# Turned cache pages for the compression stage of a decoder-layer kernel

## The reference, cut to what matters

```
sub = kv[:, :n_sub * 16].reshape(b, n_sub, 16, 2, 2, 64)            # 16 tokens j of each sub-block n
for r in range(2):
    part_r = einsum("bnjcgd,cjde->bncge", sub + pe_r, cmp_w[:, 16 r : 16 r + 16])[:, r:r + n_cmp]
blk = part_0 + part_1                                                # 127 blocks of a sequence, 31 of the prompt
kc, vc = rmsnorm(blk[:, :, 0], gain), blk[:, :, 1]
```

## Time and profile before

| what | us |
|---|---|
| median of three runs | 1944.69 |
| time of the profiled execution | 1945.8 |
| its span | 1943.9 |
| end of stage 1 (last ACT work) | 183.3 |
| stage 2, first SP issue to last PE work | 184.5 to 300.2 |
| PE busy, 185 to 300.4 | 111.1 |
| POOL busy, 185 to 300.4 | 7.5 |

### The profile page before, as it was taken

The page is one execution under the profiler, slowest core; times in us unless marked ns, Lnnn a source line. Parts: engine busy times, 40 slices in busy tenths (PEclk is TensorE's granted clock), DMA queues, the critical chain, the costliest instruction groups (busy, mean ns, idle before and its releaser), DMA issues.

```text
span 1943.9 us, 40081 instructions
## 1 busy us (share of the span) xinstructions
PE 1807.3 (93%) x16517; PEld 970.7 (50%) x16517; DVE 577.7 (30%) x1401; ACT 366.2 (19%) x791; POOL 376.9 (19%) x434
## 2 busy tenths in 40 slices
PE   7998996778899999988999999999999999999992
PEld 4546984554478887443434444443444444343431
DVE  2223324356401111253222313232222313232324
ACT  3232442355400000110111111111111111111110
POOL 0010101137500000601121222222121212222222
PEclk9997997889799999987999999999999999999996
DMA  8205933550051110223999999999999999999986
GB/s 298 102 11 208 404 106 135 213 201 1 26 202 55 55 43 23 113 111 154 404 428 420 418 423 414 424 426 422 419 419 419 413 427 415 423 418 415 423 351 237
DMA packets 59185, 535.47 MB, mean 275 GB/s; under 512 B 15825, under 2 KB 20785, under 8 KB 44114
## 3 DMA queue, kind: packets, MB, share of 16 engines
q1 hardware_dynamic: 47465, 483.30, 60.9%
q0 software_dynamic: 11664, 51.42, 6.7%
HBM read 518.26 MB, written 28.39 MB: 281 GB/s over the span
## 4 chain that ended last, share of the span: by engine, by line
PE 52%; DMA 1%; DVE 1%; issue 0%; POOL 0%; SPq 0%; POOLq 0%; ACT 0%; DVEq 0%
PE psum L2727 34%; PE psum L2753 17%; DMA arena<-y_of 1%; DMA arena<-scr_h,arena 1%; PE psum L2737 0%; DVE arena L2714 0%; DVE arena L2720 0%; POOL arena L2626 0%; DMA y_of<-arena 0%; DVE arena L2719 0%; SPq L2574 0%; DVE arena L2663 0%; SPq L2576 0%; POOL arena L2596 0%; POOLq L2535 0%
## 5 line engine op out<-in xcount | busy, mean ns | idle before, releaser
L2727 PE MATMUL psum<-arena 128*32 128x512 f32 x6144 | 668.3, 592 | 3.6 <-DVE arena L2663 2.4
L2727 PEld LDWEIGHTS psum<-arena 128*32 128x32 f32 x6144 | 210.0, 108 | 442.9 <-issue 438.5
L2753 PE MATMUL psum<-arena 128*32 128x256 f32 x6144 | 343.8, 378 | 0.0
L2753 PEld LDWEIGHTS psum<-arena 128*32 128x32 f32 x6144 | 211.8, 109 | 134.0 <-issue 12.6
L2688 DVE TENSOR_TENSOR arena<-psum,arena 128x512 f32<-128x512 f32 x96 | 66.4, 692 | 576.5 <-PE psum L2727 543.9
L2613 POOL DMA_INDIRECT y_of<-arena x96 | 96.9, 1009 | 475.3 <-ACT arena L2649 475.3
L2376 PE MATMUL psum<-arena 128*128 128x272 f32 x768 | 183.0, 396 | 1.6 <-PEq L224 1.6
L2376 PEld LDWEIGHTS psum<-arena 128*128 128x128 f32 x768 | 146.9, 191 | 35.3 <-issue 3.2
L2645 ACT ACTIVATE arena<-arena 128x256 f32<-128x256 f32 x96 | 40.1, 418 | 611.2 <-DVE arena L2690 598.3
L745 PE MATMUL psum<-arena 128*128 128x512 f32 (+3 forms) x320 | 112.2, 509 | 0.2 <-DVE arena L617 0.2
L2592 POOL DMA_INDIRECT arena<-scr_h,arena x96 | 98.9, 1030 | 48.9 <-POOL arena L2588 28.1
(11 more groups left out here) (360 smaller groups left out, 1544.9 us busy)
## 6 DMA issues: line engine op xcount, KB each, us to landing
arena<-in_w_gu SPq DMA_DIRECT2D x64, 4096.0 KB
arena<-in_w_down SPq DMA_DIRECT2D x32, 4096.0 KB
arena<-in_w_gb SPq DMA_DIRECT2D x24, 512.0 KB, 3.5
arena<-y_of SPq DMA_DIRECT2D x8, 1024.0 KB, 14.2
arena<-in_w_tok SPq DMA_DIRECT2D x3, 2048.0 KB, 17.6
arena<-in_x_all SPq DMA_DIRECT2D x8, 512.0 KB, 11.1
arena<-in_cache_mem SPq DMA_DIRECT2D x8, 512.0 KB, 11.7
arena<-in_cache_win SPq DMA_DIRECT2D x8, 512.0 KB, 11.8
```

The lines of the kernel that those rows point to most:

```text
L2727: mm = pe.matmul(gu_bank(g)[32 * j:32 * j + 32].rearrange("p (h n) -> p h n", h=2), xgT[:, g, 32 * k:32 * k + 32], gu_w(slot)[:, part, :, ...
L2753: mm = pe.matmul(dn_half(g)[32 * j:32 * j + 32], actT[:, g, 32 * k:32 * k + 32], dn_w(slot)[:, part, 256 * j:256 * j + 256], start=(k == 0 ...
```

## The change

The cache in HBM is laid out by page, turned: row (page, a, d) of 1 KB holds (c j g m), with m the eight sub-blocks of the page. The 128 rows of a page are then 128 partitions, and a sequence is 16 pages of 128 rows of 1 KB. The columns that a product reads are 32 runs of 8 words, 256 words apart between pages. No turn on PE and no copy to `kvT` is left for the sequences; the prompt's rows still go that way.

SP issues 9 of the 16 pages of each sequence, each with a row number read into a register from SBUF; POOL issues the other 7 as indirect transfers. There are three buffers (the third lies behind the page numbers, where stage 1's pooling data and `kvT` were), and for each buffer two semaphores. Sequences 0 and 1 are issued in stage 1: by SP between L482 and the writes of the tables, by POOL at the old place.

```diff
+PAGES = PAST // PAGE
+PAGE_W = 2 * PAGE
+BY_SP = 9
-    cc = a["cache_cmp_kv"][0].reshape(-1, SUB // 2, 2, 2, 2, HD)
-    f["cache_cmp"] = cc.transpose(0, 3, 1, 4, 2, 5).reshape(-1, ROWF)
+    cc = a["cache_cmp_kv"][0].reshape(-1, PAGE // SUB, SUB // 2, 2, 2, 2, HD)
+    f["cache_cmp"] = cc.transpose(0, 3, 6, 4, 2, 5, 1).reshape(-1, PAGE_W)
+    f["page_list"] = np.asarray(a["page_table"]).reshape(1, -1)
...
+        sub_buf = lambda s: sub_rows[:, s % 3] if s % 3 < 2 else arena[:, third_at:third_at + ROWF]
+        page_of = lambda buf, pg: buf[:, PAGE_W * pg:PAGE_W * pg + PAGE_W]
+        def load_pages(sp, s):
+            for pg in range(BY_SP):
+                at = PAGES * s + pg
+                first = sp.value_load(page_row[0:1, at:at + 1], min_val=0, max_val=n_rows - 128)
+                sp.dma_start(page_of(sub_buf(s), pg), i["cache_cmp"][bass.ds(first, 128)]).then_inc(s_sub[s % 3], 16)
+        def gather_pages(pool, s):
+            for pg in range(BY_SP, PAGES):
+                at = PAGES * s + pg
+                pool.indirect_dma_start(page_of(sub_buf(s), pg), None, i["cache_cmp"],
+                                        bass.IndirectOffsetOnAxis(page_row[:, at:at + 1], 0)).then_inc(s_subw[s % 3], 16)
...
                 sp.dma_start(pages, i["pages"]).then_inc(s_pg, 16)
+                sp.dma_start(page_list, i["page_list"].partition_broadcast(128)...).then_inc(s_pg, 16)
...
+                sp.wait_ge(s_ix, 2)
+                for s in range(2):
+                    load_pages(sp, s)
                 for h in range(NH):            # the writes of the tables
...
+                dve.tensor_scalar(page_row, page_list, float(PAGE), cols[:, 0:1], ALU.mult, ALU.add).then_inc(s_ix, 1)
```

```diff
+                tokens(0)          # waits for all parts of sequence 7 and the prompt's rows
+                blocks(NS - 1)
+                tokens(1)
+                keys(NS - 1)
+                for c in range(2):
+                    products(NS, c)
                 blocks(NS)
                 keys(NS)
```

More of the change, by code:

```diff
@@ L312, in build_program @@
         row_index = take(NS, dt=U32)
+        page_row = take(NS * PAGES, dt=U32)
+        after_pages = cursor[0]
         u_prompt = take(2, 16 + NP_TOK)
@@ L336, in build_program @@
         s_ix = sem("s_ix")
-        s_sub = [lasting(f"s_sub{n}") for n in range(2)]
+        page_list = sub_rows[:, 1, 0:NS * PAGES].bitcast(I32)
+        s_sub = [lasting(f"s_sub{n}") for n in range(3)]
+        s_subw = [lasting(f"s_subw{n}") for n in range(3)]
         s_const = sem("s_const")
@@ L839, in build_program @@
         phase_over()
-        cursor[0] = phase_base + 16
+        assert cursor[0] >= third_at
+        cursor[0] = third_at + ROWF
         pe_bias = take(2)
-        kvT = take(2, 8, 2, 128)
         parts = take(2, 2, 128)
@@ L966, in _ @@
                     load_window(sp, 0, s)
-                sp.wait_ge(s_ct, 8 * 7)
+                for s in range(5, NS):
+                    sp.wait_ge(s_cw_mm, 2 * (s - 2))
+                    load_pages(sp, s)
+                sp.wait_ge(s_cw_mm, 2 * 6)
                 for c in range(2):
@@ L978, in _, with copy_group, sum_bank @@
                 for s in range(2, NS):
[L979 to L989, removed]
+                    if s >= 3:
+                        pool.wait_ge(s_cw_mm, 2 * (s - 2))
+                    gather_pages(pool, s)
+                for s in range(2):
+                    gather_selected(pool, 0, s)
+            def copy_group(eng, copy, c, q):
+                n = subs(NS)
+                eng.wait_ge(s_cw_mm, 2 * 7)
+                eng.wait_ge(s_ct, 4 * c + q + 1)
                 copy(kvT[:, c, 2 * q:2 * q + 2, :, 0:n], bank(q)[:, 0:4 * n].rearrange("p (j g n) -> p j g n", j=2, g=2)
                      ).then_inc(s_kv[q], 1)
+            def sum_bank(s, c):
+                return bank((4 if s % 2 == 0 else 2) + c)
             @block.scalar
@@ L1011, in after, with keys_in @@
                     act.activation(kc_rt[0:n], kc_ss[0:n], ACT.Sqrt, bias=eps[0:n], scale=1.0 / HD).then_inc(s_kr, 1)
+                def keys_in(s):
+                    n = subs(s) - 1
                     act.wait_ge(s_kt, s + 1)
                     act.activation(kcT[:, s, 0:n], bank(7)[:, 0:n], ACT.Copy).then_inc(s_kc, 1)
[L1015 to L1031, removed]
@@ new lines, in blocks_in @@
+                def blocks_in(s, c):
+                    act.wait_ge(s_cw_mm, 2 * s + c + 1)
+                    if s:
+                        act.wait_ge(s_bl, s)
+                    n = subs(s)
+                    sums = sum_bank(s, c)[:, 0:2 * n].rearrange("p (g n) -> p g n", g=2)
+                    for r in range(2):
+                        q = slice(64 * r, 64 * r + 64)
+                        act.activation(parts[q, c, :, 0:n - 1], sums[q, :, r:r + n - 1], ACT.Identity,
+                                       bias=pe_bias[q, c:c + 1]).then_inc(s_pa, 1)
@@ new lines, in _ @@
+                for s in range(NS):
+                    blocks_in(s, 0)
+                    if s:
+                        after(s - 1)
+                    blocks_in(s, 1)
+                    if s:
+                        keys_in(s - 1)
+                for q in (0, 2):
+                    copy_group(act, cp, 0, q)
+                after(NS - 1)
+                for q in (0, 2):
+                    copy_group(act, cp, 1, q)
+                keys_in(NS - 1)
+                for c in range(2):
+                    blocks_in(NS, c)
@@ L1032, in _ @@
                 after(NS)
+                keys_in(NS)
             @block.vector
@@ L1052, in after @@
                     dve.tensor_tensor(kn[0:n], kn[0:n], gain_kc[0:n], ALU.mult).then_inc(s_kn, 1)
[L1054 to L1059, removed]
+                for s in range(NS - 1):
+                    after(s)
+                for q in (1, 3):
+                    copy_group(dve, cp, 0, q)
+                after(NS - 1)
+                for q in (1, 3):
+                    copy_group(dve, cp, 1, q)
                 after(NS)
@@ L1118, in keys @@
                     pe.transpose(bank(7)[:, 0:n], kn[0:n], ident[0:n, 0:n]).then_inc(s_kt, 1)
-                for s in range(NS + 1):
-                    tokens(s, 0)
+                for s in range(NS):
+                    products(s, 0)
                     if s:
                         blocks(s - 1)
-                    tokens(s, 1)
+                    products(s, 1)
                     if s:
                         keys(s - 1)
-                    for c in range(2):
-                        products(s, c)
+                tokens(0)
+                blocks(NS - 1)
+                tokens(1)
+                keys(NS - 1)
+                for c in range(2):
+                    products(NS, c)
                 blocks(NS)
```

58 lines of the change are left out of this document (36 added, 22 removed).

## The result

The changed kernel takes 1948.7 us (median of 20 runs, 1941.5 to 1953.3), the kernel before 1943.4 (20 runs, 1938.6 to 1946.8): a ratio of 1.0026, 95% interval 1.0017 to 1.0035. It is slower by 5.4 us, where 9.0 us less had been forecast (1935.7). The time is within the range that was given, and on the other side of no change.

What follows compares the result with a forecast made beforehand. PE bounds stage 2 before the change, SP's page issues after it. Stage 2 ending at 290.6 against 300.2 gains 9.6 us, less 0.6 for the clock: -9.0 us, forecast 1935.7 us, range 1919 to 1953.

Steps and rivals of the forecast that it cites:

- Turns removed: PE in stage 2: 7.9 us a sequence against 11.68, 30 us over 8 sequences if data is always there.
- rival C: Stage 2 products read slower on runs of 8 words; if their 6.90 us doubled, 29 us slower, 1974; chance 0.03.
- SP the bound: SP's nine page issues take 10.35 us a sequence in stage 2, more than PE's 7.9, so SP sets the pace.
- A page's price: One SP page by register, value load to issue: 1.15 us, between 0.75 and 1.48.
- Rival B: SP's page costs more, gain gone at 1.275 us a page; at 1.39 the kernel takes 1953 us; chance 0.23.
- The border: Between stages 1 and 2: SP's pages delay the table writes, so stage 2 begins at 188.7, 4.2 us late.
- The last page of sequence 7 is issued at 264.5 and lands about 2.4 us later: SP's chain in stage 2: sequence 7's data is there at 266.9, and the stage ends at 290.6.
- tail: Stage 2 after sequence 7's products: 16.0 us, from the old 14.8 of prompt and tail plus 1.2.
- they cost nothing: The selected gathers, moved behind POOL's last pages to about 255 us and needed after 290, cost nothing.
- Hidden: Stage 2 transfers: a sequence's 2.1 MB needs 6.3 us instead of 5.2, below PE's 7.9, so hidden.
- The clock: PE waits about 2.5 us a round in stage 2, which may lower its clock; 0.6 us taken off the gain.
- Rival A: SP's page is cheap (0.90 us), PE or POOL sets the pace; stage 2 ends at 275.1, 1920 us; chance 0.22.

Runs made afterwards that it cites:

- e1_selected_late: The changed kernel with the two selected gathers held until the first products of sequence 7 are done: 1934.3 us, ratio 0.9953 to the kernel before.
- e4_data_there: The changed kernel without the loads of sequences 3 to 7, which compute on the pages of 0 to 2: 1920.3 us, ratio 0.9880 to the kernel before.
- e10_pages_act: e9 with ScalarE issuing two of SP's nine pages of sequences 3 to 7: 1915.8 us, ratio 0.9855 to the kernel before.
- e7: e1_selected_late with SP issuing the pages of sequences 2 to 7 and the prompt rows before everything else of stage 2: 1934.8 us, ratio 0.9953 to the kernel before.
- e5: The changed kernel with SP's pages read from fixed rows, without the register read: 1927.7 us, ratio 0.9921 to the kernel before.
- e9: e8 with ScalarE issuing gate scratch, constants and gate rows at the start of stage 2: 1926.3 us, ratio 0.9913 to the kernel before.
- e8: e7 with SP's pages of sequence 1 issued at the start of stage 2, not in stage 1: 1933.8 us, ratio 0.9947 to the kernel before.

## Why the prediction was wrong

**Right.** *Turns removed*: 7.96 us for a round (7.9). *Products on runs of 8 words* cost nothing: a group of 16 records takes 214.78 - 211.24 = 3.54 us from its start to the next instruction's, two groups 7.1, against 6.90, so rival C is out. The Trainium skill, SBUF — State Buffer, Specifications (TRN2), has lines of 16 bytes that want at least two reads each for the full rate. The trace agrees. *SP the bound, SP's wait last at the border, PE idle before sequences 3 to 7 until SP's last page had landed*: so it was.

**A page's price: right, a little high.** 1.12 us from page to page in stage 1, 1.09 without the few long ones, against 1.15. Rival B had the sign of the result, 1953 us and a chance of 0.23, but not its cause: its condition was a page of 1.275 us or more, and only the nine of sequence 3 cost that (223.9 - 212.3 = 11.6 us for eight steps, 1.45 each). The value load itself took 0.270 us by median in stage 1. The Trainium skill, DMA: Bandwidth & Descriptors, Latency and other measured facts, gives about 600 ns as the floor of `tensor_load`. The trace disagrees: its page loads reached that only among the nine of sequence 3 (0.691 us by median).

**The border: 1.7 us too early** (190.4, predicted 188.7). SP's first value load began at 158.8, not 157.8, since the page list landed only at 158.3; the 18 pages took 20.4 us from there (predicted 20.7), and the last table landed at 188.0 (predicted 187.5). The two pool outputs behind the tables had been left out, and SP's last wait ended at 188.5, 1.0 us late. From there to its first issue of stage 2 it was 2.0 us, not 1.24: the other 0.7.

**The step that failed: "The last page of sequence 7 is issued at 264.5 and lands about 2.4 us later".** The miss of the stage's end, 305.5 - 290.6 = 14.9 us, taken apart (rounded):

| term | predicted | measured | difference |
|---|---|---|---|
| last page of 7 issued | 264.5 | 268.9 | 4.4 (1.7 of it the border, 2.5 the pages of 3) |
| from issue to landing | 2.4 | 9.3 | 6.9 |
| landing to the end of 7's products | 7.7 | 11.1 | 3.4 (2.9 the slow first group) |
| tail | 16.0 | 16.3 | 0.3 |

The landing time came from eight transfers of the prompt's rows with no page and no gather beside them. The trace of before had the other case too: one of its window loads of 512 KB, issued at 206.4 us with gathers in flight, landed 20.2 us later. The same text moved the selected gathers to 255 us and said that "they cost nothing", because they are needed late. Their own delay costs nothing; what they do to the pages issued behind them was not asked. e1_selected_late is the test: with the gathers out of the way the landing is 2.0 us, the first group 3.72, stage 2 ends 10.1 us earlier, and the sign of the result turns. The issue times were the same, so this is what those gathers cost there. "Hidden" was argued from the mean (6.3 us of transfer in a round of 7.9), while from 210 to 250 us spill, memory, window and two sequences of pages were in flight at once and the engines were full.

**The clock: a term too small.** 0.6 us was taken off; the slow groups of sequences 3 and 7 alone are 1.5 + 2.9 = 4.4 us, 2.9 of them on the last chain. The two long waits were over 7 us, where the text assumed about 2.5 in each round.

**Rival A** was wrong for this kernel, but its stage end of 275.1 is about what the stage takes when no page is late: 277.3 in e4_data_there, which begins the stage 5 us late, and 273.5 in e10_pages_act.

What stays open: which part of the wait before sequence 3 belongs to the late issues (212.3 to 223.9) and which to the landing (7.3 us by median, 11.4 at most); e7 removed both at once. Nor was the value load's rise to 0.69 us by median in that stretch tried by itself. And the last page of sequence 7 landed 3.2 us behind the page before it and 3.7 us behind the second gather, while five of the eight prompt transfers that SP issued behind it had already landed. Whether those, issued later, would have held it up a little too was not tried.

## What to carry to other kernels

When an edit multiplies the issues of a load, write down for the last one that a consumer waits for what else is in flight at that moment, also transfers of other queues that are needed much later; put these behind it. Then spread the issues over every queue that has room, and count everything that the issuing engine still has to do before the block's end: in e7 a gain of 9.7 us shrank to 0.9 at the barrier. A landing time is a figure for the load beside it, so take it from a stretch as full as the one that is forecast. And before a gain is told from two profiled executions, compare the stages that the edit doesn't touch: here one of them differed by 4 us of its own.

## What the runs showed of the hardware

- A 128 KB page in 1 KB rows landed in 2.0 us at the least with little beside it (e1, 255 to 269 us) and in 7.1 to 11.7 us beside two gathers of 2.1 MB in 16 KB rows.
- A value load on SP took 0.270 us by median in stage 1 and 0.691 (at most 1.03) from 211 to 223 us, while the spill of 2.2 MB was under way. Full DMA engines alone did not do it: from 226 to 269 us, at a share of up to 1.05, the loads took 0.28 us. In e7, where the spill comes behind the pages, the 54 loads of stage 2 took 0.44 us at most. The view of that line in the kernel after:

```profile
L436 SPq TENSOR_LOAD <-arena x18: 264/270/467, 158.8 to 178.1; - x18
```

```profile
L436 SPq TENSOR_LOAD <-arena x9: 267/691/1029, 211.4 to 223.1; - x9
```

- In stage 2, behind idle times of 3.9 us (e5) to 8.6 us, PE's next group of products took 5.15 to 6.65 us in place of 3.7 each time, at a lower granted clock (0.85 on average from 230 to 240 us in the kernel after). Behind those of 2 to 3 us it did in some (2.14 us in e9, then 5.39 for a group; 2.57 in e8, then 5.22) and not in others (2.95 in e8, 2.50 in the kernel after, then 3.72).
- ScalarE took 21 issues (scratch, constants, gate rows) and 10 pages with their value loads, and PE's rounds didn't lengthen (7.96 us in e10).
